# Post-norm of a two-block transformer kernel: gain multiplied in when the banks are emptied, squares taken from the banks, one add for the residual, two stores

## The reference

```python
def _rms(x, g):
    y = x * lax.rsqrt(jnp.mean(x * x, axis=-1, keepdims=True) + EPS)
    return y * g

for l in range(2):
    mod = silu(c) @ w_ada[l] + b_ada[l]            # 6 x 1024 numbers for x, the same for xc from c_ctx
    sh_a, sc_a, gt_a, sh_f, sc_f, gt_f = split(mod, 6)
    h = _rms(x, g_attn_pre[l]) * (1.0 + sc_a) + sh_a
    ...                                            # projections and three kinds of attention
    y = merged @ w_out[l]
    x = x + gt_a * _rms(y, g_attn_post[l])         # post-norm "a"
    if l == 0: xc = xc + cgt_a * _rms(yc, g_attn_post[l])
    hf = _rms(x, g_ffn_pre[l]) * (1.0 + sc_f) + sh_f
    x = x + gt_f * _rms(swiglu(hf), g_ffn_post[l]) # post-norm "f"
    if l == 0: xc = xc + cgt_f * _rms(swiglu(hfc), g_ffn_post[l])
return x
```

## Time and profile before

| | us |
|---|---|
| median of 3 runs | 2495.97 (2494.44 to 2498.8) |
| profiled execution | 2496.97 |
| its span | 2495.2 |
| PE busy | 2213.4 (89% of the span) |
| DVE busy | 1733.8 (69%) |
| ACT busy | 1155.1 (46%) |
| POOL busy | 52.6 (2%) |

### The profile page before, as it was taken

How to read it: one execution, slowest core, us unless ns; L and a number is a source line. 1 busy time by engine, 2 the same in 40 slices (tenths; PEclk the granted TensorE clock), 3 DMA queues, 4 the chain that set the end, 5 groups by cost and what they waited for, 6 DMA issues and landing times.

```text
span 2495.2 us, 38036 instructions
## 1 busy us (share of the span) xinstructions
PE 2213.4 (89%) x14746; PEld 1989.0 (80%) x14746; DVE 1733.8 (69%) x3402; ACT 1155.1 (46%) x1907; POOL 52.6 (2%) x65
## 2 busy tenths in 40 slices
PE   3998799999999999998968789699989988797997
PEld 2987799999987778887857476699879977567997
DVE  5667678889977777778775565677676665664554
ACT  2543444555554444544444345444454445354443
POOL 1000000000000000000000000000000000000000
PEclk9999899999999999989978769899999998898999
DMA  7648546654467777766622100477657843103664
GB/s 275 202 141 277 186 153 197 212 186 149 148 225 260 261 258 240 247 211 219 223 83 96 34 18 18 137 241 245 223 189 251 255 147 122 51 1 102 186 186 119
DMA packets 137971, 435.04 MB, mean 174 GB/s; under 512 B 15360, under 2 KB 38144, under 8 KB 137280
## 3 DMA queue, kind: packets, MB, share of 16 engines
q1 hardware_dynamic: 109424, 396.93, 49.6%
q10 hardware_dynamic: 25776, 23.97, 2.8%
q0 software_dynamic: 2592, 11.70, 1.3%
HBM read 418.91 MB, written 13.63 MB: 173 GB/s over the span
## 4 chain that ended last, share of the span: by engine, by line
PE 56%; DVE 17%; issue 10%; DMA 10%; ACT 5%; POOL 1%; ACTq 0%; POOLq 0%; SPq 0%; DVEq 0%
PE bk L1657 54%; DVE SPL L1089 4%; DMA TMP<-kept 3%; PE bk L1663 3%; DVE R L1089 2%; DMA RAW<-in_win 2%; DVE RAW L1123 2%; ACT SPL L744 1%; DVE R L1098 1%; ACT R L746 1%; DMA HID<-kept 1%; DMA RAW<-in_peer 1%; DMA kept<-TMP 1%; DVE ST L1104 1%; ACT R L744 1%
## 5 line engine op out<-in xcount | busy, mean ns | idle before, releaser
L1089 DVE TENSOR_TENSOR SPL<-RAW,SPL 128x1024 fp32r<-128x1024 f32 (+1 forms) x614 | 744.8, 1218 | 366.6 <-ACT SPL L744 365.3
L744 ACT ACTIVATE SPL<-RAW 128x1024 fp32r<-128x1024 f32 (+1 forms) x614 | 645.3, 1054 | 617.3 <-PE bk L1657 337.0
L1657 PE MATMUL bk<-HH,SPL 128*128 128x256 f32 x3840 | 747.8, 288 | 22.5 <-DVE SPL L1089 14.0
L1657 PEld LDWEIGHTS bk<-HH,SPL 128*128 128x128 f32 x3840 | 620.6, 194 | 28.1 <-ACT SPL L744 12.6
L1657 PE MATMUL bk<-SPL,WHL 128*128 128x512 f32 x2328 | 555.2, 392 | 16.3 <-DVE WHL L1089 10.3
L1657 PE MATMUL bk<-HL,SPL 128*128 128x256 f32 x1920 | 547.0, 285 | 0.0
L1657 PEld LDWEIGHTS bk<-SPL,WHL 128*128 128x128 f32 x2328 | 428.4, 188 | 111.5 <-issue 23.4
L1657 PEld LDWEIGHTS bk<-HL,SPL 128*128 128x128 f32 x1920 | 372.3, 194 | 2.7 <-issue 0.2
L1657 PE MATMUL bk<-SPL,HH 128*128 128x256 f32 (+1 forms) x1664 | 320.8, 295 | 41.1 <-DVE SPL L1089 26.6
L1657 PEld LDWEIGHTS bk<-SPL,HH 128*128 128x128 f32 x1664 | 273.6, 202 | 49.9 <-issue 29.4
L744 ACT ACTIVATE R<-bk 128x512 f32<-128x512 f32 (+5 forms) x376 | 186.1, 508 | 255.6 <-PE bk L1657 225.2
(11 more groups left out here) (126 smaller groups left out, 1957.3 us busy)
## 6 DMA issues: line engine op xcount, KB each, us to landing
RAW<-in_peer SPq DMA_DIRECT2D x256, 512.0 KB, 4.7
RAW<-in_ada SPq DMA_DIRECT2D x144, 512.0 KB, 4.8
RAW<-in_ffn SPq DMA_DIRECT2D x132, 512.0 KB, 4.2
RAW<-in_win SPq DMA_DIRECT2D x96, 512.0 KB, 4.6
RAW<-in_ffd SPq DMA_DIRECT2D x66, 512.0 KB, 4.2
RAW<-in_wout SPq DMA_DIRECT2D x32, 512.0 KB, 4.5
kept<-TMP ACTq DMA_DIRECT2D x88, 128.0 KB, 3.2
TMP<-kept ACTq DMA_DIRECT2D x66, 128.0 KB, 5.6
```

Source lines behind the costliest of these rows:

```text
L744: ins = e.activation(out, in_, func, bias=bias, scale=scale)
L1089: e.tensor_tensor(out, a, b, op).then_inc(*dve.up(*points))
L1657: ins = e.matmul(out, lhsT, rhs, start=start, stop=stop, skip_group_check=True)
```

## The change

There are four edits.

1. **Post-norm.** The bank is no longer copied: DVE multiplies it with the gain row on its way to oY. ACT squares and sums straight from the bank, in pieces, so the two squares over oY are gone. For op, ACT's squares wait until DVE has read the bank; for the network's four banks DVE starts with banks 0 and 1 and ACT with 2 and 3. DVE adds the partial sums with one small reduction. The two operations of 128 x 1024 for each half become one, x = oY * r + x.
2. **Plan.** sil3 comes behind the context's first op step and ahead of its second; the ada steps start only with the context's feed-forward network (24 there, 24 in the main stream's, as before). sil2 is put 16 steps ahead of the end of the attention.
3. **Banks.** A bank of fo is free when both DVE and ACT have read it.
4. **Store.** Each half of the output is stored as soon as its x is there.

```diff
-    last = [("sil2", 1), ("sil3", 1)] + ada_steps(l1, range(48))
+    last = ada_steps(l1, range(48))
...
-    plan += weave(chain + qkv_steps(0, 0, True), attend_steps(0, 1)) + attend_steps(0, 0)
-    side = weave(out_steps(0, 1) + pre_steps(0, 1) + ffn_steps(0, 1), last[:26])
+    rows = attend_steps(0, 0)
+    plan += weave(chain + qkv_steps(0, 0, True), attend_steps(0, 1)) + rows[:-16] + [("sil2", 1)] + rows[-16:]
+    side = out_steps(0, 1)[:3] + [("sil3", 1)] + out_steps(0, 1)[3:] + pre_steps(0, 1) + weave(ffn_steps(0, 1), last[:24])
...
-            sp.wait_ge(T.at("x3", 1, 0, "f"))
-            e.dma_start(out_d.rearrange("b (i p) d -> p (b i) d", p=P), LX[0]).then_inc(*T.up("d_out", 16, [("stored",)]))
+            for i in range(2):
+                sp.wait_ge(T.at("x3" if i else "x3a", 1, 0, "f"))
+                e.dma_start(out3[:, i, :], LX[0][:, i, :]).then_inc(*T.up(f"d_out{i}", 16, [("stored", i)]))
...
# ACT
             def op(l, s, j):
                 key = ("op", l, s, j)
-                act.wait_ge(T.at("full", key))
-                A(v2(QS[(l, s)]["oY"], 2)[:, :, j * 256:(j + 1) * 256], v2(ps(*key), 2), ACT.Copy, ("out", key))
-            def an_a(l, s, k):
-                ...
-                squares(v2(q["oY"], 2), stat(8, 2, s), q["junk"][:, 0:1024], ("an_s", l, s, k))
+                act.wait_ge(T.at("scaled", key))
+                for i in range(2):
+                    A(..., ps(*key)[:, i * 256:(i + 1) * 256], ACT.Square, ..., accum=stat(40 + 4 * i + j, 1, s))
...
             def fo(l, s):
-                for i in range(2):
-                    A(v2(QS[(l, s)]["oY"], 2)[:, i, 512:1024], ps(*key), ACT.Copy, ("out", key))
+                for c in (2, 3, 0, 1):
+                    act.wait_ge(T.at("full", ("fy", l, s)) if c >= 2 else T.at("scaled", key))
+                    A(..., ps(*key), ACT.Square, ("squared", key), ("an_s", l, s, "f"), accum=...)
...
# DVE
+            def op(l, s, j):
+                dve.wait_ge(T.at("full", key), T.at("gB", l, s, "a", 1))
+                tt(v2(QS[(l, s)]["oY"], 2)[:, :, c], v2(ps(*key), 2),
+                   QS[(l, s)]["gB"][:, c].unsqueeze(1).to_broadcast([P, 2, 256]), ALU.mult, ("scaled", key))
             def an_a(l, s, k):
                 dve.wait_ge(T.at("an_s", l, s, k))
+                rsum(stat(8, 2, s), parts, ALU.add)
                 mean_eps(stat(8, 2, s), D, "an", l, s, k)
             def an_b(l, s, k):
                 newton(r, y, a, "an", l, s, k)
                 for i in range(2):
-                    stt(yi, yi, r[:, i:i + 1], q["gB"], ALU.mult, ALU.mult)
-                    tt(LX[s][:, i, :], LX[s][:, i, :], yi, ALU.add, ("x3" if i else "x3a", l, s, k))
+                    stt(LX[s][:, i, :], v2(q["oY"], 2)[:, i, :], r[:, i:i + 1], LX[s][:, i, :], ALU.mult, ALU.add, ...)
             def fo(l, s):
-                    cp(v2(QS[(l, s)]["oY"], 2)[:, i, 0:512], ps(*key), ("out", key))
+                for c in range(4):
+                    dve.wait_ge(T.at("full", ("fy", l, s)) if c < 2 else T.at("squared", key), T.at("gB", l, s, "f", 1))
+                    tt(v2(QS[(l, s)]["oY"], 2)[:, c // 2, h], ps(*key), QS[(l, s)]["gB"][:, h], ALU.mult, ("scaled", key))
```

More of the change, by code:

```diff
@@ L1035, in op @@
                 key = ("op", l, s, j)
-                act.wait_ge(T.at("full", key))
-                A(v2(QS[(l, s)]["oY"], 2)[:, :, j * 256:(j + 1) * 256], v2(ps(*key), 2), ACT.Copy, ("out", key))
-            def an_a(l, s, k):
-                q = QS[(l, s)]
-                if k == "f":
-                    act.wait_ge(T.at("out", ("fy", l, s, 2)))
-                squares(v2(q["oY"], 2), stat(8, 2, s), q["junk"][:, 0:1024], ("an_s", l, s, k))
+                act.wait_ge(T.at("scaled", key))
+                for i in range(2):
+                    A(QS[(l, s)]["junk"][:, 512 * j + 256 * i:512 * j + 256 * i + 256], ps(*key)[:, i * 256:(i + 1) * 256], ACT.Square,
+                      *([("out", key), ("an_s", l, s, "a")] if i else []), accum=stat(40 + 4 * i + j, 1, s))
             def an_b(l, s, k):
@@ L1060, in fo @@
             def fo(l, s):
-                for i in range(2):
-                    key = ("fy", l, s, 2 * i + 1)
-                    act.wait_ge(T.at("full", ("fy", l, s)))
-                    A(v2(QS[(l, s)]["oY"], 2)[:, i, 512:1024], ps(*key), ACT.Copy, ("out", key))
+                for c in (2, 3, 0, 1):
+                    key = ("fy", l, s, c)
+                    act.wait_ge(T.at("full", ("fy", l, s)) if c >= 2 else T.at("scaled", key))
+                    A(QS[(l, s)]["junk"][:, 512 * c:512 * c + 512], ps(*key), ACT.Square,
+                      ("squared", key), ("an_s", l, s, "f"), accum=stat(40 + 4 * (c // 2) + c % 2, 1, s))
             steps = {"sil": sil_, "sil3": sil3, "norm_a": norm_a, "nT": nT, "mix_in": mix_in, "qk": qk, "decay": decay,
@@ L1588, in dT @@
                 tt(H[s][1][:, 2:4, :], v2(ps(*key), 2), H[s][0][:, 2:4, :].bitcast(F32), ALU.subtract, ("out", key))
+            def op(l, s, j):
+                key, c = ("op", l, s, j), slice(j * 256, (j + 1) * 256)
+                dve.wait_ge(T.at("full", key), T.at("gB", l, s, "a", 1))
+                tt(v2(QS[(l, s)]["oY"], 2)[:, :, c], v2(ps(*key), 2),
+                   QS[(l, s)]["gB"][:, c].unsqueeze(1).to_broadcast([P, 2, 256]), ALU.mult, ("scaled", key))
             def an_a(l, s, k):
+                parts = v2(stat(40, 8, s), 2)[:, :, 0:4 if k == "a" else 2]
                 dve.wait_ge(T.at("an_s", l, s, k))
+                rsum(stat(8, 2, s), parts, ALU.add)
+                dve.wait_ge(dve.own)
                 mean_eps(stat(8, 2, s), D, "an", l, s, k)
@@ L1613, in fo @@
             def fo(l, s):
[L1614 to L1617 removed]
+                for c in range(4):
+                    key, h = ("fy", l, s, c), slice(512 * (c % 2), 512 * (c % 2) + 512)
+                    dve.wait_ge(T.at("full", ("fy", l, s)) if c < 2 else T.at("squared", key), T.at("gB", l, s, "f", 1))
+                    tt(v2(QS[(l, s)]["oY"], 2)[:, c // 2, h], ps(*key), QS[(l, s)]["gB"][:, h], ALU.mult, ("scaled", key))
             steps = {"A1": a1, "A2": a2, "mods": mods_, "norm_a": norm_a, "norm_k": norm_k,
@@ L1651, in take @@
                 if b in held:
-                    pe.wait_ge(T.at("out", held[b]))
+                    pe.wait_ge(*([T.at("squared", held[b]), T.at("scaled", held[b])] if held[b][0] == "fy" else
+                                 [T.at("out", held[b])]))
                 held[b], T.bank[key] = key, b
```

17 lines of the change are left out of this document (7 added, 10 removed).

## The result

| | before | after |
|---|---|---|
| median, us | 2496.59 (2494.44 to 2498.8) | 2466.1 (2461.65 to 2469.53) |
| profiled execution | 2496.97 | 2466.55 |
| its span | 2495.2 | 2464.8 |

The ratio is 0.9877, with a 95% interval of 0.9858 to 0.9895. Two repetitions of the changed kernel gave 0.9891 (0.9876 to 0.9906) and 0.9884 (0.9869 to 0.9899). The time is inside the forecast range of 2463 to 2481, 3.9 us under the 2470.

What follows compares the result with a forecast made beforehand. PE's six stalls, 56.7 us, behind post-norm chains or splits after them, bound it. 9.2 + 3.4 + 3.2 + 4.1 + 3.35 + 3.3 - 1 = 25.6 us off 2496.97: 2471.4, 2470 as median; range 2463 to 2481.

Steps and rivals of the forecast that it cites:

- Part 1: All six post-norms: one operation for two per half brings the last x 2.46 us earlier, all reaching PE.
- Part 2: Layer 1, op's evacuation and sums: 2.10 us instead of 3.00; with the earlier x, stall 13.18 falls by 3.35.
- Part 3: Context's ops: silu and ada steps moved, stall 7.55 becomes 1.4 us, the fifth op ends 8.7 us earlier.
- Part 4: Context's last op bank: DVE multiplies it 2.8 us late, so 9.2 us are gained over stalls 7.55 and 13.22.
- What it adds: Context's feed-forward network: ops holding up DVE and ACT, and four more ada chunks, cost 1 us, bounds 0 and 9.4.
- the second and third rival: Context's network: PE stalls a few times, 8 us back, 2478, chance 0.18; or round after round, 2502, chance 0.02.
- Part 5, stall 3.80: Main stream's post-norm "a", layer 0: shorter chain and one ada product less ahead save 3.4 us, bounds 2.4 and 3.8.
- Part 5, stalls 9.91 and 9.02: Post-norm "f" of context and main stream: shorter chains and earlier squares save 3.2 and 4.1 us.
- Part 6: Kernel's end: faster evacuation, earlier last x and a last half store landing in 3.7 us save 3.3 us.
- The slower case: Network: DVE's wait for a full bank stalls PE round after round, 31 us lost, 2502; chance 0.02.
- no change: At each stall something else is last, such as the gain row or POOL, so shorter chains gain nothing; chance 0.03.
- The case for 2465: Context's last op bank: DVE is not late, stall 9.02 gives 5, no extra costs: 31 us won; chance 0.15.

Runs made afterwards that it cites:

- the experiment: Changed kernel with an extra 128 x 1024 DVE operation put back ahead of each residual one, at all six post-norms: 2482.4 us, ratio 0.9962 against the kernel before.
- the third trace of the changed kernel: The changed kernel run once more with no edit, beside a repetition of the kernel before: 2465.09 us, ratio 0.9884.
- the run with the ada steps later: Changed kernel with the first four steps of the context's feed-forward network put ahead of the ada steps: 2459.96 us.
- the plan alone: Kernel before with only sil2, sil3 and the ada steps in their new places: 2488.39 us, ratio 0.9977.
- one store: Changed kernel with a single output store of 1 MB behind the last x, in place of two halves: 2458.76 us.

## Why the prediction was right, point by point

The sum was 25.6 us and the stretch gave 25.66. That is better than its terms deserve: several were off, and by luck they cancelled. That the medians differ by 30.5 us and not 25.6 is no merit of the forecast either; 4.75 us of the first pair of traces lie in code that the change doesn't touch.

**Part 1 (one operation for two): right.** 2.48 us for two operations where I had 2.54, and 14.6 us over six post-norms by the experiment, 14.8 by mine.

**Part 2 (evacuation of op): right, a little small.** Stall 13.18 became 9.46, 3.72 less, against 3.35. The step that was dearer in my sum was the squares: 0.37 us of pace each from the bank, not 0.53. Multiplying from the bank took DVE 0.69 us, as the row of SBUF numbers had it; the bound "twice its row" did not come.

**Part 3 (the silu and the ada steps): right, a little large.** 8.10 us instead of 8.7, with a stall of 1.12 instead of 1.4. The 8.10 are 6.43 us of stall and 1.66 of busy time at the higher clock (1.9 forecast). The term that was too small is the ops' own time: the 144 matmuls of ops three to five took 16.87 us at full clock (15.74 to 32.61 behind the split), not 16.2. ACT in order of time, which answers to the earlier trace rows:

```profile
1554.12 1.28 ACT L747 ACT_TABLE_LOAD   x1
1555.41 1.92 ACT L747 ACTIVATE TMP<-TMP 128x2048 f32<-128x2048 f32 x1
1557.23 1.04 ACT L747 ACTIVATE SPL<-RAW 128x1024 fp32r<-128x1024 f32 x1
```

The silu starts 0.01 us behind the load again, and the stall is under the 1.4 us I had without a drain. The further drain of some 1380 ns that the Trainium skill gives (ScalarE: Activation LUTs, What ACT_TABLE_LOAD costs) is not seen here; by the page it would have been 2.8. The clock came as forecast too: behind this short stall it was at full speed (1.00). Behind the next, long one it was at half (first two columns: stretch and its length; PEclk is third from the end):

```profile
1587.70:1591.70 4.00, 4.00 (x18) 3.70 (x19) 1.98 (x5) 2.09 (x5) 0.00 (x0) 0.50 0.00 0
1561.00:1577.00 16.00, 15.54 (x135) 15.35 (x134) 9.78 (x11) 8.43 (x18) 0.00 (x0) 1.00 0.63 209
```

**Part 4 (DVE late at the fifth bank): the mechanism right, its size too large.** DVE in order of time:

```profile
1575.97 1.22 DVE L1123 CUSTOM_DVE_ANT_0 RAW<-RAW,TMP 128x1024 f32<-128x1024 f32 x1
...
1577.12 1.22 DVE L1089 TENSOR_TENSOR SPL<-RAW,SPL 128x1024 fp32r<-128x1024 f32 x1
1578.26 0.68 DVE L1089 TENSOR_TENSOR R<-bk,R 128x512 f32<-128x512 f32 x1
1579.84 0.16 DVE L1104 TENSOR_REDUCE ST<-ST 128x2 f32<-128x8 f32 x1 [0.91 <-ACT R L749]
```

The bank is full at 1576.54 and is multiplied at 1578.26, 1.7 us late and not 2.8. The shorter squares are part of the difference, since they stood in that chain twice. So 10.16 us were won up to the transposes, not 9.2.

**What it adds: twice what I booked, and the cause another.** The 1 us I booked for extra work in the context's network came out as 2.0 (10.16 less 8.17 in the table), and most of it is the clock; that the table stands at my 8.2 there is part 4's surplus of 1 us. The stretch from the first matmul of that network to its next stall, before and then after (stretch, its length, busy time with instruction count of PE first, PEclk third from the end):

```profile
1612.01:1749.04 137.03, 137.02 (x1020) 130.55 (x1020) 100.50 (x132) 62.21 (x84) 0.70 (x1) 1.00 0.72 231
```

```profile
1597.11:1736.12 139.01, 138.68 (x1020) 132.02 (x1020) 104.34 (x142) 63.95 (x94) 0.80 (x1) 0.99 0.73 231
```

The same 1,020 matmuls took 1.66 us more; in the first 10 us the granted clock was 0.83 (71 matmuls) where it had been 1.00 (85). In the third trace of the changed kernel these 1.5 us are not there (137.17), so they are no fixed cost of the change. They may be more likely with it: both traces of the kernel before are free of them, and of the ten traces of edited kernels only two are (that third one and the run with the ada steps later). In the plan alone the stretch took 138.53 us. One new idle piece of 0.33 us is in all three traces; the moved ada work alone doesn't explain it, since the plan alone has none. The fear behind the second and third rival, a network that stalls round after round, had nothing to it.

**Part 5, stall 3.80: wrong.** The step that failed is "the order puts one ada product less ahead of it". It puts two more there, directly ahead of the low part. DVE of the changed kernel, in order of time:

```profile
1734.67 0.42 DVE L1089 TENSOR_TENSOR WHL<-R,WHL 128x256 fp32r<-128x256 f32 x1 [1.53 <-ACT WHL L747]
1735.01 1.22 DVE L1123 CUSTOM_DVE_ANT_0 R<-RAW,TMP 128x1024 f32<-128x1024 f32 x1
...
1736.15 1.22 DVE L1123 CUSTOM_DVE_ANT_0 RAW<-RAW,TMP 128x1024 f32<-128x1024 f32 x1
...
1737.30 1.22 DVE L1089 TENSOR_TENSOR SPL<-RAW,SPL 128x1024 fp32r<-128x1024 f32 x1
```

The plan adds 1.26 us (3.80 to 5.06) and the shorter chain takes 2.51 (5.06 to 2.55), so 1.25 us of stall went and not 3.4. That the place has gained 3.2 us when the next stall begins is luck, as far as my sum goes: the 524 matmuls between kept PE busy for 73.76 us instead of 75.52, at a granted clock of 1.00 instead of 0.98. This goes with the stall in all twelve traces: behind one of 3.38 to 5.06 us (four traces) that stretch had 0.97 or 0.98, behind one of 0.86 to 2.55 us (eight traces) 1.00. The stretch before and then after:

```profile
1752.83:1829.48 76.65, 75.52 (x524) 70.52 (x524) 51.93 (x75) 37.03 (x56) 0.70 (x1) 0.98 0.70 226
```

```profile
1738.67:1813.33 74.66, 73.76 (x524) 68.94 (x524) 54.59 (x82) 35.88 (x57) 1.39 (x2) 1.00 0.74 246
```

I had counted the steps in the plan, not read DVE's order at the very instruction that released PE.

**Part 5, stalls 9.91 and 9.02: the stalls right, the clock left out.** 3.63 went (3.2 forecast) and 4.4 (4.1). But behind the shorter stalls the same matmuls ran slower: behind the first, 1,386 of them kept PE busy for 197.42 us instead of 196.28, and behind the second, 128 for 20.74 instead of 18.68. With the next stall also longer (1.39 before, 2.02 now), the second place kept some 2 us of its 4.4. This is most of the 3.2 us by which the table falls behind the forecast at the stall of 13.18. That shorter stalls cause the lower clock is not shown: in the plan alone, where both stalls have their old length, the two stretches take 197.54 and 20.46 us, and with one store, where both have the new length, the second takes 18.46. So the clock behind a stall does not follow from that stall's length alone; what else it follows is open.

**Part 6 (the end): right in kind, too small.** 4.8 us instead of 3.3. ACT, DVE and SP in order of time:

```profile
2454.92 0.60 ACT L749 ACTIVATE R<-bk 128x512 f32<-128x512 f32 x1 [6.55 <-PE bk L1664]
2454.92 2.48 DVE L1089 TENSOR_TENSOR R<-bk,R 128x512 f32<-128x512 f32 x4 [5.26 <-PE bk L1664]
...
2457.37 0.16 DVE L1104 TENSOR_REDUCE ST<-ST 128x2 f32<-128x4 f32 x1
...
2459.13 2.48 DVE L1098 SCALAR_TENSOR_TENSOR R<-R,ST 128x1024 f32<-128x1024 f32 x2
2460.44 1.54 SPq L637 DMA_DIRECT2D out<-R  x2
```

Four squares of 512 from banks and DVE's four multiplications run beside each other, and both are through in 2.4 to 2.5 us, where I had let ACT be the slower one: 1.1 us saved up to the store's issue and not 0.5. The last store landed in 2.7 us, below my bounds of 2.8 and 4.0; the 3.7 that I took is the term of this part that was mis-sized by most. The fit in the Trainium skill (DMA: Bandwidth & Descriptors, Anatomy of one DMA), 2.0 us fixed and 436 GB/s, fitted on the GpSimd path, makes 3.2 us of 512 KB and 4.4 us of 1 MB, which are estimates from that page. The stores here took 2.7 and 4.0 us, both less, so the 4.0 us do not fit the page as well as I had written, though its 3.2 came nearer than my 3.7.

**The rest of the difference** to the forecast is open. The medians of before and after lie 27.7 to 30.5 us apart in three comparisons, each good to 4 or 5 us, and the stretch accounts for 25.6 to 27.2. Whether the part ahead, where the split lay at 1548.69 and 1548.29 in the old kernel and at 1538.72 to 1550.20 in the new, is faster by 1 or 2 us on average, five traces don't tell. The slower case and no change were rightly given little. The case for 2465 has the nearer time, but not for its reasons: DVE was late.

## What to carry to other kernels

Read the order of the engine that releases the stall, at the very instruction that releases it, and count what stands directly ahead of it in the new order; the number of steps in the plan says nothing about that. Filler work (here the ada products) costs nothing until it stands between a chain's last link and the split that PE waits for: four steps further back took 2.5 us off PE's idle time, and the distance fell by 3.6 to 5.1 us, of which the rest is the clock's play. Where a distance falls by more than the idle time does, look at the busy time of equal matmuls before crediting the edit. Where the clock plays by some microseconds, compare two kernels from the last instruction that they share to the end, and time a candidate before believing a gain of 0.2%.

## What the runs showed of the hardware

- Over twelve traces of all kernels the unchanged code came to the same instruction anywhere within 14 us (1536.19 to 1550.20), with 42 to 84 matmuls in the same 12 us at a granted clock of 0.50 to 1.00. From there to the end, executions of one kernel agreed to 0.03 us (before, two traces) and 1.6 us (after, three traces).
- Behind the stall that was 3.80 us before, the next 524 matmuls ran at a granted clock of 0.97 to 0.98 in the four traces with a stall of 3.38 to 5.06 us, and of 1.00 in the eight with 0.86 to 2.55 us. Ahead of the context's network the same stall of 2.3 us was followed by 10 us at 0.83 in two traces of the changed kernel and at 1.00 in the third.
- ACT squared a 128 x 256 piece of a bank, with the sum, in 0.38 us (the SBUF row has 417 ns) at a pace of 0.37 us, and a 128 x 512 bank in 0.60 us at a pace of 0.57.
- DVE's multiplication from a bank (0.69 us for 512 numbers) was no slower than from SBUF. DVE and ACT read different banks at the same time with no visible loss: 2.48 us for four multiplications, against 0.69 for one alone.
- A store of 512 KB behind another took 2.7 us to land, one of 1 MB 4.0.
